# Norms between sub-layers: squares of the last four tiles summed on TensorE, halves for the last tile, the diagonal, the spread and one weight split

## The reference

```python
def rms_norm(x, g):
    xf = x.astype(jnp.float32)
    y = xf * lax.rsqrt(jnp.mean(xf * xf, axis=-1, keepdims=True) + NORM_EPS)
    return (y * g.astype(jnp.float32)).astype(x.dtype)

def ada_pre(h, g, shift, scale):
    return rms_norm(h, g) * (1.0 + scale) + shift

def swiglu(u, w_in, w_out):
    gate, val = jnp.split(u @ w_in, 2, axis=-1)
    return (jax.nn.silu(gate) * val) @ w_out

for l in range(DEPTH):
    h = h + 0.5 * gate_0 * swiglu(ada_pre(h, norm_g[l, 0], shift_0, scale_0), ffn_w_in[l, 0], ffn_w_out[l, 0])
    h = h + gate_1 * mixer_l(ada_pre(h, norm_g[l, 1], shift_1, scale_1))
    h = h + 0.5 * gate_2 * swiglu(ada_pre(h, norm_g[l, 2], shift_2, scale_2), ffn_w_in[l, 1], ffn_w_out[l, 1])
out = rms_norm(h_lat, final_g)
```

## Time and profile before

| | us |
|---|---|
| median of 3 runs | 2022.41 |
| lowest, highest | 2022.39, 2024.84 |
| the profiled execution, its own time | 2026.71 |
| its span, first to last instruction | 2024.7 |
| PE busy | 1966.8 (97%) |
| DVE busy | 1222.5 (60%) |
| ACT busy | 645.8 (32%) |
| mean granted clock of PE, share of 2.4 GHz | 0.986 |

### The profile page before, as it was taken

The page is one execution under the profiler, slowest core; times in us unless marked ns, Lnnn a source line. Parts: engine busy times, 40 slices in busy tenths (PEclk is TensorE's granted clock), DMA queues, the critical chain, the costliest instruction groups (busy, mean ns, idle before and its releaser), DMA issues.

```text
span 2024.7 us, 25021 instructions
## 1 busy us (share of the span) xinstructions
PE 1966.8 (97%) x9588; PEld 1580.9 (78%) x9588; DVE 1222.5 (60%) x1615; ACT 645.8 (32%) x662; POOL 85.5 (4%) x169
## 2 busy tenths in 40 slices
PE   8899999999999999999999999999999999899999
PEld 3588888877876777888888688888877777499998
DVE  5877666568558757677655966333373346764445
ACT  4621222232331133212223322122243356443343
POOL 0011010000000000010000001000000010000000
PEclk9899999999999999999999999999999999999999
DMA  9255555422230014555543355222312213044552
GB/s 340 93 207 197 177 206 177 136 103 73 94 119 1 33 63 164 189 197 190 194 148 122 112 188 198 104 88 99 137 63 78 78 63 126 21 146 166 186 182 109
DMA packets 48321, 271.64 MB, mean 134 GB/s; under 512 B 5380, under 2 KB 6148, under 8 KB 24840
## 3 DMA queue, kind: packets, MB, share of 16 engines
q1 hardware_dynamic: 28536, 194.30, 26.9%
q0 software_dynamic: 19728, 76.55, 11.2%
HBM read 269.79 MB, written 1.05 MB: 134 GB/s over the span
## 4 chain that ended last, share of the span: by engine, by line
PE 88%; DVE 7%; ACT 2%; issue 1%; DMA 1%; SPq 0%; DVEq 0%; ACTq 0%
PE ps L1393 26%; PE ps L1394 25%; PE ps L1395 25%; PE ps L1674 2%; PE ps L1386 2%; DVE tn L877 2%; PE ps L1754 1%; DVE act_lo L863 1%; PE ps L1664 1%; PE ps L1839 1%; DMA edecay<-log_decay_dram 1%; ACT w_hi L403 1%; DVE w_lo L787 1%; PE ps L1717 1%; ACT act_hi L431 0%
## 5 line engine op out<-in xcount | busy, mean ns | idle before, releaser
L1393 PE MATMUL ps<-act_hi,w_hi 128*128 128x512 f32 (+1 forms) x2728 | 986.6, 362 | 16.7 <-DVE w_lo L787 7.4
L1394 PE MATMUL ps<-act_lo,w_hi 128*128 128x512 f32 (+1 forms) x2728 | 980.2, 359 | 0.0
L1395 PE MATMUL ps<-act_hi,w_lo 128*128 128x512 f32 (+1 forms) x2728 | 980.1, 359 | 0.0
L787 DVE TENSOR_TENSOR w_lo<-w_raw,w_hi 128x2048 fp32r<-128x2048 f32 x172 | 394.0, 2290 | 491.6 <-ACT w_hi L403 491.6
L1393 PEld LDWEIGHTS ps<-act_hi,w_hi 128*128 128x128 f32 x2728 | 516.7, 189 | 107.9 <-DVE act_lo L863 12.4
L1395 PEld LDWEIGHTS ps<-act_hi,w_lo 128*128 128x128 f32 x2728 | 516.8, 189 | 76.1
L1394 PEld LDWEIGHTS ps<-act_lo,w_hi 128*128 128x128 f32 x2728 | 517.0, 190 | 75.2 <-issue 0.5
L403 ACT ACTIVATE w_hi<-w_raw 128x2048 fp32r<-128x2048 f32 x172 | 329.1, 1914 | 627.8 <-PE ps L1395 627.8
L803 DVE SCALAR_TENSOR_TENSOR ada_w<-ada_w,cond_bc 128x1024 f32<-128x1024 f32 x128 | 156.0, 1219 | 0.0
L803 DVE SCALAR_TENSOR_TENSOR ada_prod<-ada_w,cond_bc 128x1024 f32<-128x1024 f32 x128 | 155.9, 1218 | 0.0
L443 ACT ACTIVATE silu_g<-ps 128x1024 f32<-128x1024 f32 (+1 forms) x44 | 40.5, 920 | 307.3 <-PE ps L1395 307.2
(11 more groups left out here) (216 smaller groups left out, 1085.8 us busy)
## 6 DMA issues: line engine op xcount, KB each, us to landing
w_raw<-w_stream_dram SPq DMA_DIRECT2D x172, 1024.0 KB, 4.8
ada_w<-ada_rows_dram POOLq DMA_DIRECT2D x128, 512.0 KB, 3.7
ada_raw<-ada_stream_dram POOLq DMA_DIRECT2D x4, 1024.0 KB, 12.3
ada_in<-ada_stream_dram POOLq DMA_DIRECT2D x4, 1024.0 KB, 16.5
bd<-bd_dram SPq DMA_DIRECT2D x4, 768.0 KB, 6.2
edecay<-log_decay_dram SPq DMA_DIRECT2D x4, 512.0 KB, 10.3
h<-tokens_dram SPq DMA_DIRECT2D x1, 2048.0 KB, 12.7
wg<-wg_dram SPq DMA_DIRECT2D x3, 512.0 KB, 4.5
```

Source lines behind the costliest of these rows:

```text
L787: dve.tensor_tensor(w_lo[:, g % 2, :], w_raw[:, g % 2, :], w_hi[:, g % 2, :].bitcast(F32), ALU.subtract).then_inc(w_lo_done, 1)
L1393: pe.matmul(out, wh, xh, start=start, stop=False)
L1394: pe.matmul(out, wh, xl, start=False, stop=False)
L1395: return pe.matmul(out, wl, xh, start=False, stop=stop)
```

## The change

The last four tiles are no longer added by DVE. ACT writes their squares to the four `tn` buffers, and PE sums them: behind the four matmuls on `sq_sum`, which now holds tiles 0 to 3, come four for each of tiles 4 to 7, accumulated into one column in each of banks 0 to 3. For 512 tokens that is 20 matmuls with one moving column where there were 4; for 256 tokens it is 10 where there were 2. The last tile is squared in halves. The diagonal and the spread of norms 1 to 4 are made in halves, in banks 5 and 6. DVE's subtraction of the next weight block is made in halves too, the first behind the update of tile 0, the second where the whole one stood. Of the 14 `keep_warm` matmuls of a norm, 2 are left between sums and spread, and 2 behind. `w_used` is now set by the last matmul on `sq_sum`. Norm 0 and the buffers of the weights are as before.

```diff
+        def rb_half(n, c):
+            if 0 < n < 5:
+                return ps[:, 5 if c == CTXC else 6, 0:256]
+            return ps[:, 6 if n else 4, c]
+        def ss_col(n, t, w):
+            return ps[:, t:t + w, 0] if n else ps[:, 0, t:t + w]
+        def sq_tile(m):
+            return sq[:, m % 2] if m < 4 else tn[:, m - 4]
...
                 for m in range(KT):
+                    if 2 <= m < 4:
+                        act.wait_ge(sq_added, 3 * (n - 1) + 1)
+                    if m == KT - 1 and cols == ALLC:
+                        act.wait_ge(h_half, n)
+                        act.activation(sq_tile(m)[:, CTXC], h[:, m, CTXC], ACT.Square).then_inc(sq_half, 1)
+                        act.wait_ge(h_ready, 8 * n + m + 1)
+                        act.activation(sq_tile(m)[:, LATC], h[:, m, LATC], ACT.Square).then_inc(sq_ready, 1)
+                        continue
                     act.wait_ge(h_ready, 8 * n + m + 1)
-                    if m >= 2:
-                        act.wait_ge(sq_added, 7 * (n - 1) + max(m - 2, 1))
-                    act.activation(sq[:, m % 2, cols], h[:, m, cols], ACT.Square).then_inc(sq_ready, 1)
+                    act.activation(sq_tile(m)[:, cols], h[:, m, cols], ACT.Square).then_inc(sq_ready, 1)
...
+            def split_half(g, half):
...
+                dve.wait_ge(w_hi_done, g + 1)
+                c = slice(1024 * half, 1024 * half + 1024)
+                ins = dve.tensor_tensor(w_lo[:, g % 2, c], w_raw[:, g % 2, c], w_hi[:, g % 2, c].bitcast(F32),
+                                        ALU.subtract)
...
-                split_w(NORM_BLOCKS[n])
+                split_half(NORM_BLOCKS[n], 1)
                 rms_diag(n, cols)
...
-                        if m >= 2:
+                        if m == 0:
+                            split_half(NORM_BLOCKS[o + 1], 0)
+                        if 2 <= m < 5:
                             add_squares(o + 1, m - 1, cols)
-                    add_squares(o + 1, KT - 1, cols)
...
             def square_sums(n, cols):
...
-                    mm = pe.matmul(ps[:, 0, t:t + 1], sq_sum[:, c], col("mean_w"), start=True, stop=True)
+                    mm = pe.matmul(ss_col(n, t, 1), sq_sum[:, c], col("mean_w"), start=True, stop=n == 0)
...
+                mm.then_inc(w_used, 1)
+                for m in range(4, KT):
+                    for t in range((cols.stop - cols.start) // P):
+                        if m == KT - 1 and t == 0 and cols == ALLC:
+                            pe.wait_ge(sq_half, n)
+                        elif t == (2 if m == KT - 1 and cols == ALLC else 0):
+                            pe.wait_ge(sq_ready, 8 * (n - 1) + m + 1)
+                        c = slice(cols.start + t * P, cols.start + t * P + P)
+                        mm = pe.matmul(ss_col(n, t, 1), sq_tile(m)[:, c], col("mean_w"), start=False, stop=m == KT - 1)
                 mm.then_inc(ss_done, 1)
...
+                if 0 < n < 5:
+                    pe.wait_ge(diag_half, n)
+                    pe.matmul(rb_half(n, CTXC), ones[:], diag[:, 0:2, :], start=True, stop=True).then_inc(rb_half_ready, 1)
+                    pe.wait_ge(diag_ready, n + 1)
+                    pe.matmul(rb_half(n, LATC), ones[:], diag[:, 2:4, :], start=True, stop=True).then_inc(rb_ready, 1)
+                    return
...
             def chain(n, cols):
-                pe.wait_ge(h_ready, 8 * n + 6)
-                keep_warm(5, 3).then_inc(w_used, 1)
-                pe.wait_ge(h_ready, 8 * n + 8)
-                keep_warm(7, 3)
+                pe.wait_ge(sq_added, 3 * n)
                 square_sums(n, cols)
-                keep_warm(7, 5)
+                keep_warm(7, 2)
                 rms_rows(n, cols)
-                keep_warm(7, 3)
+                keep_warm(7, 2)
```

More of the change, by code:

```diff
@@ L418, in root @@
                 act.wait_ge(ss_done, n + 1)
-                act.activation(cols4[:, 0, 0:w], ps[:, 0, 0:w], ACT.Sqrt, bias=col("eps_norm")).then_inc(std_ready, 1)
+                act.activation(cols4[:, 0, 0:w], ss_col(n, 0, w), ACT.Sqrt, bias=col("eps_norm")).then_inc(std_ready, 1)
             def affine(n, cols):
@@ L788, in split_w @@
                                   ALU.subtract).then_inc(w_lo_done, 1)
+            def split_half(g, half):
+                if g >= N_BLOCKS:
+                    return
[3 more added lines that the diff above has]
+                                        ALU.subtract)
+                if half == 1:
+                    ins.then_inc(w_lo_done, 1)
             def ada_bias(q):
@@ L845, in rms_diag @@
                 dve.wait_ge(rstd_ready, n + 1)
-                dve.tensor_tensor(diag[:, 0:w, :], ident[:].rearrange("p (a c) -> p a c", a=1).to_broadcast([P, w, P]),
-                                  cols4[:, 1, 0:w].rearrange("p (t a) -> p t a", a=1).to_broadcast([P, w, P]),
-                                  ALU.mult).then_inc(diag_ready, 1)
+                halves = [slice(0, 2), slice(2, 4)] if 0 < n < 5 else [slice(0, w)]
+                for t in halves:
+                    size = [P, t.stop - t.start, P]
+                    ins = dve.tensor_tensor(diag[:, t, :], ident[:].rearrange("p (a c) -> p a c", a=1).to_broadcast(size),
+                                            cols4[:, 1, t].rearrange("p (t a) -> p t a", a=1).to_broadcast(size), ALU.mult)
+                    ins.then_inc(diag_ready if t.stop == w else diag_half, 1)
             def scaled(n, cols, final=False):
-                dve.wait_ge(rb_ready, n + 1)
-                rb = rb_bank(n)
+                dve.wait_ge(*((rb_half_ready, n) if 0 < n < 5 else (rb_ready, n + 1)))
                 if not final:
@@ L869, in scaled @@
                     if final:
-                        dve.scalar_tensor_tensor(out_sb[:, k, :], h[:, k, cols], col("final_g", k), ps[:, rb, cols],
+                        dve.scalar_tensor_tensor(out_sb[:, k, :], h[:, k, cols], col("final_g", k), rb_half(n, cols),
                                                  ALU.mult, ALU.mult).then_inc(out_ready, 1)
@@ L876, in scaled @@
                         if c.start >= cols.start:
+                            if k == 0 and c == LATC and n > 0:
+                                dve.wait_ge(rb_ready, n + 1)
                             last = dve.scalar_tensor_tensor(tn[:, k % 4, c], h[:, k, c], coef_a[:, n, k, cd:cd + 1],
-                                                            ps[:, rb, c], ALU.mult, ALU.mult)
+                                                            rb_half(n, c), ALU.mult, ALU.mult)
                     last.then_inc(tn_ready, 1)
@@ L971, in rest @@
                                                                 h[:, m, c], ALU.mult, ALU.add)
+                                if m == KT - 1 and c == CTXC:
+                                    last.then_inc(h_half, 1)
                         last.then_inc(h_ready, 1)
-                        if m >= 2:
+                        if m == 0:
+                            split_half(NORM_BLOCKS[o + 1], 0)
+                        if 2 <= m < 5:
                             add_squares(o + 1, m - 1, cols)
-                    add_squares(o + 1, KT - 1, cols)
                 return first, rest
@@ L1461, in square_sums @@
                 mm.then_inc(ss_done, 1)
             def rms_rows(n, cols):
+                w = (cols.stop - cols.start) // P
+                if 0 < n < 5:
[3 more added lines that the diff above has]
+                    pe.matmul(rb_half(n, LATC), ones[:], diag[:, 2:4, :], start=True, stop=True).then_inc(rb_ready, 1)
+                    return
```

18 lines of the change are left out of this document (8 added, 10 removed).

## The result

| | before | after |
|---|---|---|
| median of the runs made side by side (12 each), us | 2024.63 | 2029.78 |
| lowest, highest | 2022.39, 2027.39 | 2027.4, 2033.61 |
| the profiled execution, time and span | 2026.71, 2024.7 | 2028.77, 2026.9 |
| mean granted clock of PE | 0.986 | 0.980 |

The ratio after to before is 1.0023, with a 95% interval of [1.0016, 1.0030]: 4.7 us slower (3.2 to 6.1). The forecast was +1.4 us, inside what counts as no change, and 2023.8 us with a range up to 2027.8. So the sign was that of the forecast and the size was not. Another 2.2 us of the miss is the base: 2022.41 was the median of three runs, of a kernel whose twelve runs have a median of 2024.63. Without these 2.2 us the 2029.78 would be 2027.56, just inside the range that ended at 2027.8.

What follows compares the result with a forecast made beforehand. The prediction took PE's matmuls and its waits at the six norms as the bound. Long norms cost 5.6 us net of their gain, short norms gain 4.2: +1.4 on 2022.4 gives 2023.8 us, range 2014.3 to 2027.8.

Steps and rivals of the forecast that it cites:

- The stream of loads: Sums of norms 1 to 4: 40 weight loads take 4.56 us, bound the root, and bring it 0.88 us later.
- The gain of a long norm without a fall: Norms 1 to 4, 512 tokens: second `tn` starts 0.7 us earlier each if PE's clock stays up, 2.9 us for four.
- That the clock falls in each long norm: Norms 1 to 4: narrow matmuls without wide moving columns let PE's clock fall once each, price taken as 2.1 us.
- its 22 loads: Case of a fall 2 us into a long norm's stream: 22 loads at the slow clock pay 2.3 us.
- The short norms: Norms 5 and 6, 256 tokens: gain 2.1 us each, nothing charged for the clock, upper bound 0.5 each.
- rival C: Norm 5's squares come late through the wait for `w_hi`: it gains 1.4 us, not 2.1; no separate chance given.
- the forecast's lower bound: Norm 5's gain, taken as 2.1 us, was given bounds from 1.4 to 2.6.
- -7.1 without falls: All six norms with the clock up: 2.9 us gained in norms 1 to 4 and 4.2 in norms 5 and 6.
- +8.4 for the long norms: Price of the clock falls in norms 1 to 4, taken as 2.1 us each before their gain of 0.7 each.
- A slow first block costs nothing: First weight block behind a norm: PE has slack, since it idled 1.29 us behind norm 2 for the next split.
- A (clock up): Rival: the dense stream of loads keeps PE's clock up in the norms; 2015.3 us, chance 0.33.
- B (early in every norm, and down through the spread): Rival: clock falls early in each long norm and stays down, price 3.9 us each; +8.6 us, 2031.0, chance 0.09.

Runs made afterwards that it cites:

- experiment 1: The changed kernel with 64 moving columns of ones instead of one column in the sums of norms 1 to 6; ratio to the kernel before 0.9969.
- experiments 10 and 11: The changed kernel with 64 moving columns in norms 1 to 4 alone, ratio to the kernel before 0.9974; in norms 5 and 6 alone, 1.0012.
- experiments 5 and 9: DVE adds to tile 5 in both: experiment 1 with PE's squares for tiles 6 and 7 only, 1.0016; ones as weights, squares moving, no diagonal or spread, 1.0013.
- experiment 7: Experiment 1 with DVE's weight split whole and at its old place; ratio to the kernel before 0.9958.

## Why the prediction was right or wrong

**The stream of loads, right.** From the last product to the root it is 4.79 us in norms 1 and 3 where it was 4.12, so the root comes 0.67 later, forecast 0.88: the loads start with the last product, 0.3 us earlier than the forecast had them. The squares bound nothing, the reciprocal stands 0.29 behind the root (0.30).

**The gain of a long norm without a fall, right.** 7.85 - 7.00 = 0.85 each in experiment 1, forecast 0.7.

**That the clock falls in each long norm, and why, right; its price, right in the profile and somewhat low over the runs.** Against experiment 1 the four norms of after paid 1.44, 2.66, 1.46 and 2.20, mean 1.9; the forecast took 2.1. The runs of the table of experiments 10 and 11 give 2.2 to 2.5. (The forecast's parts, 11 loads at 0.102 more and 0.91, give 2.03, and its 22 loads 2.24.) The parts were shared out otherwise than told: the forecast had loads and keep-warm pay and the spread little. In norms 1 and 3 the stream stayed fast. The keep-warm matmuls, 0.86 us longer, held the spread's load 0.69 later behind the last product (6.52 against 5.83), and from that load to the second `tn` it took 1.92 us against 1.17. In norm 2 loads paid too, 4.68 us for 32 against 3.65, and in norm 4 in part. The reason for the low clock is the one that the forecast took from the earlier trace rows, moving columns: experiment 1 changes nothing else in PE's program. The Trainium skill, "TensorE: Matmul & The Clock Gate", section "Why this matters for your kernels", asks only for no long idle gaps. The change itself goes against it: its clock fell behind 4.60 us in which PE was never idle. The idle wait of 1.45 us did not let the clock fall each time (experiments 5 and 9), and no run here has a longer one ahead of its sums, so none tests what the section says of long gaps.

**The short norms, wrong: the failed step.** "The short norms have 2.3 us of loads, and the spread there waits for the diagonal, so I charge nothing; the upper bound is a slow spread, 0.5 each." The clock fell in both, and they paid 0.72 and 1.08 us for it against experiment 1, both above that bound. Norm 6 of after:

```profile
2017.66 1.76 PE L1421 MATMUL ps<-cond_pad 128*32 128x256 f32 x4
...
2018.26 0.43 DVE L877 TENSOR_TENSOR diag<-ident,cols 128x256 f32<-128x256 f32 x1
...
2019.35 0.50 PEld L1516 LDWEIGHTS ps<-diag,ones 128*128 128x128 f32 x2 [0.81 <-DVE diag L877]
...
2020.61 2.83 DVE L900 SCALAR_TENSOR_TENSOR out_sb<-h,vec,ps 128x256 f32<-128x256 f32 x7 [1.93 <-PE ps L1516]
```

From the diagonal's end to `out_sb` it is 1.92 us; the forecast had 0.78. The spread did not wait for the diagonal, as the forecast had it ("Keep-warm (four instructions, 0.91) is through by then"): at the low clock the keep-warm matmuls ended at 2019.42, so the load stood 0.66 us behind the diagonal, and from load to `out_sb` it took 1.26 us, not 0.74. Without the fall (experiment 1) norm 6 gains 2.26 us, the forecast's 2.1; with it 1.18. In norm 5 a second thing failed, rival C's:

```profile
1809.34 1.23 DVE L813 TENSOR_TENSOR w_lo<-w_raw,w_hi 128x1024 fp32r<-128x1024 f32 x1 [0.74 <-ACT w_hi L414]
...
1813.56 0.52 PEld L1491 LDWEIGHTS ps<-vec,sq_sum 128*128 128x128 f32 x4 [0.72 <-DVE sq_sum L922]
```

DVE stood 0.74 us for `w_hi` with all its updates behind, and PE's sums waited for `sq_sum`. Without a fall norm 5 gains 1.39, the forecast's lower bound, and with the whole split (experiment 7) 2.04. So the short norms gave 0.67 + 1.18 = 1.85 in place of 4.2.

**The sum again, by the runs.** The forecast: -7.1 without falls, +8.4 for the long norms, 0 for the short. The runs: -6.3 (experiment 1), +9 to 10, +1 to 2. Each of the three misses has the same sign, and they make up the 3.3 us between +1.4 and +4.7. But by the runs alone no one of the three is wider than the intervals of the ratios; which term failed is read from the traces. In the one profiled pair the terms are -7.1, +7.8 and +1.8, which is 2.5 us, and the short norms' falls are the only term above the forecast. Experiment 11's long norms sum to 37.5 us where after's sum to 35.8, with the same code, so after's profile caught a mild set of falls.

**A slow first block costs nothing, right.** Behind norm 2 PE waits 1.27 us for the second split, as in the earlier trace rows, and the distances from norm 2 to 3 and from 3 to 4 are those shown above, the same before and after within 0.05 us.

**Rivals.** A (clock up) is what experiment 1 made of the kernel: ratio 0.9969 where it had 7.1 us, 0.9965. B (early in every norm, and down through the spread) held in none at its price: the clock was down through the spread in all four, but fell inside the stream in norms 2 and 4 alone, and the dearest of the four paid 2.66 us, under the 2.8 from which B would decide. What spoke for A, that a dense stream of loads may count enough, is answered by six falls in six norms.

## What to carry to other kernels

A PE that is busy without a pause can still lose its clock: 40 weight loads (20 in the short norms) with one moving column each let it fall in six norms of six, and the same loads with 64 moving columns, which took no longer (3.65 us for 32 both times), in none. That is no guarantee: with the sums cut to 24 loads (12 in the short norms) and an idle wait ahead of them, 64 columns lost the clock in four norms of six (experiment 5). Before keep-warm work is removed, count what wide work is left, in the short stages too, and price everything behind the fall: loads, the keep-warm matmuls that are left, which then stand in the way themselves, and the matmuls that the next engine waits for. In the long norms, work taken off an engine that had slack (DVE) gained nothing, and the halves and the shorter keep-warm were the gain; in the last norm, taking the adds off DVE together with the six keep-warm matmuls gained 1.06 us.

## What was not expected

- 64 moving columns in place of one left the stream of loads at 3.65 us for 32: the loads hide them.
- A load of 128 columns behind keep-warm matmuls starts only as the last of them ends (448.60 and 448.67 before, 449.58 and 449.65 after). That leaves 0.41 us without a load at the high clock and 0.81 at the low one; the releaser in the brackets of such a row is not what the load waited for.
- With the same code the clock fell at other points from run to run. Elsewhere too: the first 100 us had a mean granted clock of 0.88 before and 0.91 in experiment 1, and norm 1's last product started between 440.1 and 444.1 us; from norm 4 to norm 5 it took 311.7 to 314.5. That is of the size of the scatter of some us in each kernel's runs.
- A reciprocal of 256 columns on DVE took 1.68 us, against 0.47 for an update of the same shape.
